# Holding the row gathers of a routed-expert stage behind the dot products of two groups back

## The chip, the core and the metric

One core of one Trainium2 chip runs one program. The metric is the time of one execution on the device in microseconds; the numbers given are medians of several executions.

## What is computed

The reference runs two transformer-like blocks over 256 tokens of width 1024. The part that the change touches is the feed-forward layer of the first block: each token has 8 heads, each head picks 16 of 16384 experts, and each expert is one row of 1024 numbers in a table `peer_u` and one in a table `peer_v`.

```python
def peer_ffn(h, w_q, sub_keys, u_tab, v_tab):
    ...
    def one_block(hb):
        ...
        idx = jnp.take_along_axis(cand_i, pos, axis=-1)
        g = jax.nn.softmax(top_s, axis=-1)
        u = u_tab[idx]
        act = jax.nn.gelu(jnp.einsum('thkd,td->thk', u, hb))
        wts = (g * act.astype(jnp.float32)).astype(hb.dtype)
        v = v_tab[idx]
        return jnp.einsum('thk,thkd->td', wts, v)
```

## The kernel before

The program has four stages: the first block up to its attention and recurrent branches (to about 390 us), the expert-row stage described below (about 390 to 1170 us), the dense part of the second block (to about 1450 us), and a loop over 32 dense experts (to the end). Each engine has its own instruction list, and semaphores tie them together.

The expert-row stage works on *rows*. A row here is one pick of one head for all 128 tokens of a tile: 128 partitions times 1024 numbers of `peer_u`, and as much of `peer_v`, together 1 MB. There are 2 tiles x 8 heads x 16 picks = 256 rows, and this text counts them 0 to 255 in the order in which they are gathered. Four rows are a *group* (`GROUP = 4`), so there are 64 groups, 0 to 63; group G holds the rows 4G to 4G+3. There are 16 buffers (`uv_rows[k]`), one for each pick k of a head; row r uses buffer r mod 16.

For each row:

- POOL (GpSimd) waits until the matmuls of row r-16 have used the buffer (`s_pv`, named `v_rows_used`), then issues two indirect DMAs, one for the u half (L709) and one for the v half (L711). Both count on `uv_full[k]`.
- DVE (`dot_rows`, L1806) waits for both halves and takes the dot product of the u half with the token rows. The last dot of a group counts on `s_dots`.
- ACT (`gelu_dots`, L1164) takes the GELU of the group's four dots, DVE (`weights`, L1813) multiplies by the softmax weights, and ACT (`diagonals`, L1173) writes four diagonal matrices.
- PE (L905) multiplies each diagonal by the v half of its row and adds into PSUM, and counts on `s_pv`.

POOL runs this as a loop, `Fori`, of 4 iterations for each tile; an iteration is two heads, that is 32 rows. A head begins with a copy of its 16 indices (L697). DVE's loop over the same 32 rows is written so that it also chooses the experts for two later heads, in pieces set between the dots: `best_keys` (L1561, L1564, L1568, L1581), `best_pairs` (L1600), `soften` (L1611, L1612), `part_of_route` (L1622 to L1627). Each piece is a few short instructions with a drain between them, and stands between the dots of a group and the multiplication by the weights of that same group. The dots of the next group stand after that multiplication.

At the change of tile ACT also copies the finished tile out of PSUM (L1342).

```python
dot_rows(tile, 0, 1, i)
best_keys(after, 1)
weights(tile, 0, 1, i)
dot_rows(tile, 0, 2, i)
best_pairs(0)
weights(tile, 0, 2, i)
```

What orders POOL against DVE before the change is only `s_pv`: POOL may be up to 16 rows ahead of PE, whether or not DVE has taken their dots.

Of the kernel before, what the change touches and what calls it, by code (L numbers as in the profile page):

```python
# [35 lines left out]
PH, PK, TOPK = 8, 128, 16  # L36
# [9 lines left out]
SLOT = 4096  # L46
RING = 5
GROUP = 4
N_BANKS = 8


# [78 lines left out]
def banks_first(plan):  # L130
# [5 lines left out]
    for job in plan:  # L136
# [12 lines left out]
        else:  # L149
            at[job] = turns["early"] % N_BANKS  # L150
            turns["early"] += 1
# [83 lines left out]
class Jobs:  # L235


    def __init__(self, plan, banks, full, free, earlier=None):

        self.full, self.free = full, free  # L240
        self.base = [earlier.base[b] + earlier.uses[b] if earlier else 0 for b in range(N_BANKS)]
        self.uses = [0] * N_BANKS
        self.place = {}
# [18 lines left out]

    def all_free(self, eng, banks=range(N_BANKS)):
        for b in banks:
            eng.wait_ge(self.free[b], self.base[b] + self.uses[b])
# [41 lines left out]
def build_program(nc, a, out):  # L307
# [6 lines left out]
    with ExitStack() as ctx:  # L314
        def sem(name):
            return ctx.enter_context(nc.semaphore(name))
# [97 lines left out]
        last_row = {0: 8, 1: 15, 2: 10, 3: 12, 4: 14}  # L414
        n_groups = TOPK // GROUP

# [151 lines left out]
        s_dots = sem("dots_ready")  # L568
# [98 lines left out]
        def _(pool):  # L667
# [21 lines left out]
            for tile in range(TT):  # L689
                per = 2 * (2 + TOPK)  # L690
                with pool.Fori(0, PH // 2) as i:
                    own.enter(i, per)
                    for par in range(2):
                        g = tile * PH + par
                        pool.wait_ge(s_pv, i * (2 * TOPK) + TOPK * g + 1)
                        own.mark(pool.wait_ge(s_route, i * 2 + g + 1))  # L696
                        own(pool.tensor_copy(idx_now[:, par, :].bitcast(U32), route_idx[:, par, :].bitcast(U32)))  # L697
                        pool.sem_inc(s_taken, 1)
                        for k in range(TOPK):
                            for s, place in first_row.items():  # L700
                                if k == place:
                                    unit_free(pool, last_in_slot(s, n_first))
                            if k == 2:
                                unit_free(pool, last_in_slot(1, n_first) - RING)
                            if k == 3:
                                A.filled(pool, "ss2")
                            own.mark(pool.wait_ge(s_pv, i * (2 * TOPK) + TOPK * g + k + 2))
                            at_k = bass.IndirectOffsetOnAxis(ap=idx_now[:, par, k:k + 1].bitcast(U32), axis=0)
                            pool.indirect_dma_start(out=uv_rows[k][:, 0:D], out_offset=None, in_=a["peer_u"],  # L709
                                                    in_offset=at_k).then_inc(uv_full[k], 16)  # L710
                            pool.indirect_dma_start(out=uv_rows[k][:, D:2 * D], out_offset=None, in_=a["peer_v"],  # L711
                                                    in_offset=at_k).then_inc(uv_full[k], 16)
                own.leave(PH // 2)
# [30 lines left out]
        def _(pe):  # L744
# [163 lines left out]
            for tile in range(TT):  # L908
# [3 lines left out]
                with pe.Fori(0, PH // 2) as i:  # L912
                    for par in range(2):
                        g = tile * PH + par
                        for k in range(TOPK):
                            if k % GROUP == 0:
                                pe.wait_ge(s_diag, i * (2 * n_groups) + g * n_groups + k // GROUP + 1)
                            add(ps[:, 2 * tile, :], diag[par][:, k, :], uv_rows[k][:, D:D + 512])
# [233 lines left out]
        def _(act):  # L1152
# [7 lines left out]

            def gelu_dots(tile, par, j, i):
                some = slice(j * GROUP, (j + 1) * GROUP)
                act.wait_ge(s_dots, i * (2 * n_groups) + (tile * PH + par) * n_groups + j + 1)
                fn(dots[:, par, some], dots[:, par, some], ACT.Gelu_apprx_tanh,  # L1164
                   scale=rcol[:, 4 * tile:4 * tile + 1]).then_inc(s_act, 1)

            def diagonals(tile, par, j, i):
                g = tile * PH + par
                act.wait_ge(s_wts, i * (2 * n_groups) + g * n_groups + j + 1)
                if j == 0:  # L1170
                    act.wait_ge(s_pv, i * (2 * TOPK) + TOPK * g + 1)
                for k in range(j * GROUP, (j + 1) * GROUP):
                    last = fn(diag[par][:, k, :], ident, ACT.Copy, scale=wts[:, par, k:k + 1])  # L1173
                last.then_inc(s_diag, 1)

            for job in plan_first("ACT"):
                kind, i = job[0], job[1] if len(job) > 1 else 0
# [22 lines left out]
                elif kind == "rg":  # L1200
                    A.filled(act, *job)
                    n, j = i // 2, i % 2
# [143 lines left out]
            for job in plan_second():  # L1346
                kind, i = job[0], job[1] if len(job) > 1 else 0
# [145 lines left out]
        def _(dve):  # L1493
            own = Own(dve, s_v)
            ts, tt, stt = dve.tensor_scalar, dve.tensor_tensor, dve.scalar_tensor_tensor

            dve.wait_ge(s_cols, 16)
            dve.wait_ge(s_const, 1)
            def small_chains():
# [144 lines left out]
            for job in plan_first("DVE"):  # L1644
                kind, i = job[0], job[1] if len(job) > 1 else 0
# [113 lines left out]
                elif kind in ("brr", "bra"):  # L1759
                    if i == 0:  # L1760
                        dve.wait_ge(s_gate, KD)
                    g = 2 * i + (KD if kind == "brr" else 0)
# [39 lines left out]
            def dot_rows(tile, par, j, i):  # L1802
                g = tile * PH + par
                for k in range(j * GROUP, (j + 1) * GROUP):
                    dve.wait_ge(uv_full[k], i * 64 + 32 * (g + 1))
# [104 lines left out]
            for job in plan_second():  # L1910
                kind, i = job[0], job[1] if len(job) > 1 else 0
# [81 lines left out]
                elif kind in ("bra", "brc"):  # L1993
                    if i == 0:
                        dve.wait_ge(s_gate, KD + KD)
                    g = 2 * i + (KD if kind == "bra" else 0)
# [92 lines left out]
            with dve.Fori(0, total) as q:  # L2089
# [6 lines left out]
                g, u = g_act, u_act  # L2096
# [132 lines left out]
```

## Time and profile before

| | |
|---|---|
| median of 3 runs | 2408.35 us (2406.23 to 2408.68) |
| the profiled execution | 2423.89 us |
| its span in the trace | 2422.1 us |
| mean granted TensorE clock | 0.939 of full speed |
| busy over the span | PE 86%, PEld 49%, DVE 40%, ACT 23%, POOL 21% |
| HBM read | 782.55 MB, 324 GB/s over the span |
| gathers (queue q0) | 268.47 MB in 512 indirect DMAs |

Read busy shares by stage: the shares of the whole span mix stages that have different limits. "issue" as the releaser of an idle time means that the profile shows nothing that the engine waited for. In a timeline each row is one instruction or several merged ones, with the idle time before it in brackets.

### The profile page before, as it was taken

The numbers are of one execution on the slowest core, as the hardware profiler recorded it, in microseconds if no ns is written. First come the engines' busy times: TensorE is split into PE (matmuls) and PEld (weight loads), VectorE is DVE, ScalarE is ACT, GpSimd is POOL, SyncE is SP. The second block draws the span as 40 slices with busy tenths as digits, with TensorE's granted clock in tenths as the row PEclk, the third lists the DMA queues.
The fourth block names the chain that finished last, engine by engine and source line by source line (L and its number), as shares of the span: only waits on it lengthen the run. The fifth ranks groups of instructions, "written<-read, shape, count | busy, mean of one in ns | idle before, by whom it ended". The sixth has DMA issues, their size and how long they took to land.

```text
span 2422.1 us, 27077 instructions
## 1 busy us (share of the span) xinstructions
PE 2085.5 (86%) x8940; PEld 1175.5 (49%) x8941; DVE 971.1 (40%) x2238; ACT 568.9 (23%) x1046; POOL 499.0 (21%) x560
## 2 busy tenths in 40 slices
PE   8998998977467577487799969999999999999997
PEld 7867887622223233132478854444444444444443
DVE  5955555655566565364175241211111111111113
ACT  4635301311112111021215222222222222222221
POOL 0000003466666666566100000000000000000000
PEclk9999999988789787798899979999999999999999
DMA  7352486799999999899632419699999999999995
GB/s 296 134 214 80 190 359 258 289 367 355 356 366 359 351 362 375 338 350 359 268 146 105 174 44 413 257 429 428 429 429 429 428 428 429 429 428 429 429 429 219
DMA packets 111685, 784.31 MB, mean 324 GB/s; under 512 B 13040, under 2 KB 13296, under 8 KB 80144
## 3 DMA queue, kind: packets, MB, share of 16 engines
q1 hardware_dynamic: 37904, 515.18, 51.4%
q0 software_dynamic: 73728, 268.47, 29.1%
q8 instruction: 28, 0.46, 0.1%
q14 instruction: 25, 0.20, 0.0%
HBM read 782.55 MB, written 1.05 MB: 324 GB/s over the span
## 4 chain that ended last, share of the span: by engine, by line
PE 75%; issue 11%; DVE 6%; ACT 2%; DMA 2%; another core or an unknown queue 2%; POOL 1%; DVEq 0%; ACTq 0%; POOLq 0%; SPq 0%
PE ps L746 57%; PE ps L905 15%; DVE ring L1806 2%; PE ps L1105 1%; DMA ring<-in_peer_v,arena 1%; PE ps L878 1%; POOL ring L709 1%; DVE arena L1806 1%; POOL ring L711 1%; DMA arena<-in_peer_v,arena 1%; DVE arena L1564 0%; ACT arena L1173 0%; DVE arena L1755 0%; PE ps L1136 0%
## 5 line engine op out<-in xcount | busy, mean ns | idle before, releaser
L746 PE MATMUL ps<-ring,arena 128*64 128x512 f32 (+2 forms) x3336 | 747.5, 588 | 40.7 <-issue 40.7
L905 PE MATMUL ps<-ring,arena 128*128 128x512 f32 x768 | 373.2, 640 | 155.0 <-issue 105.8
L746 PEld LDWEIGHTS ps<-ring,arena 128*64 128x64 f32 (+1 forms) x3336 | 262.1, 140 | 499.0 <-issue 498.4
L746 PE MATMUL ps<-arena,ring 128*128 128x256 f32 x2208 | 493.0, 383 | 7.5 <-ACT arena L1367 3.7
L746 PEld LDWEIGHTS ps<-arena,ring 128*128 128x128 f32 x2208 | 420.5, 191 | 73.5 <-issue 11.4
L905 PEld LDWEIGHTS ps<-ring,arena 128*128 128x128 f32 x768 | 154.9, 206 | 369.1 <-issue 314.7
L2101 DVE TENSOR_TENSOR arena<-ps,arena 128x512 f32<-128x512 f32 x66 | 45.7, 692 | 652.6 <-PE ps L1105 652.6
L1470 ACT COPY arena<-ps 128x512 f32<-128x512 f32 (+1 forms) x198 | 108.4, 548 | 727.7 <-PE ps L746 671.6
L1806 DVE CUSTOM_DVE_ANT_0 ring<-ring,ps 128x1024 f32<-128x1024 f32 x192 | 229.0, 1218 | 118.5 <-DMA ring<-in_peer_v,arena 106.0
L905 PE MATMUL ps<-arena 64*128 64x512 f32 (+2 forms) x568 | 204.5, 613 | 73.7 <-issue 38.1
L746 PE MATMUL ps<-arena 128*128 128x128 f32 (+6 forms) x1486 | 221.6, 305 | 28.5 <-DVEq L2077 13.6
L746 PEld LDWEIGHTS ps<-arena 128*128 128x128 f32 (+2 forms) x1486 | 196.6, 198 | 45.6 <-issue 22.1
L709 POOL DMA_INDIRECT ring<-in_peer_u,arena x192 | 182.5, 950 | 145.2 <-issue 63.1
L711 POOL DMA_INDIRECT ring<-in_peer_v,arena x192 | 180.2, 939 | 59.8 <-issue 54.3
L905 PEld LDWEIGHTS ps<-arena 128*128 128x128 f32 (+1 forms) x568 | 81.3, 197 | 171.2 <-issue 129.4
L1173 ACT ACTIVATE arena<-arena 128x128 f32<-128x128 f32 x256 | 81.8, 391 | 204.3 <-issue 131.2
L1164 ACT ACTIVATE arena<-arena 128x4 f32<-128x4 f32 x64 | 19.1, 298 | 368.2 <-issue 250.4
L1806 DVE CUSTOM_DVE_ANT_0 arena<-arena,ps 128x1024 f32<-128x1024 f32 x64 | 76.4, 1219 | 35.9 <-DMA arena<-in_peer_v,arena 31.1
L697 POOL COPY arena<-arena 128x16 uint32<-128x16 uint32 x16 | 3.3, 206 | 387.5 <-POOLq L696 387.5
L709 POOL DMA_INDIRECT arena<-in_peer_u,arena x64 | 60.1, 939 | 52.4 <-PE ps L905 21.6
L711 POOL DMA_INDIRECT arena<-in_peer_v,arena x64 | 60.2, 941 | 19.6 <-issue 18.7
L1541 DVE CUSTOM_DVE_ANT_0 ring<-ring,arena 128x1024 f32<-128x1024 f32 x48 | 56.0, 1222 | 3.0 <-DVE arena L1709 0.7
(330 smaller groups left out, 1172.7 us busy)
## 6 DMA issues: line engine op xcount, KB each, us to landing
ring<-in_w_exp SPq DMA_DIRECT2D x192, 2048.0 KB, 17.1
ring<-in_w_in SPq DMA_DIRECT2D x24, 2048.0 KB, 7.8
ring<-in_w_ada SPq DMA_DIRECT2D x12, 2048.0 KB, 8.6
ring<-in_w_out SPq DMA_DIRECT2D x4, 2048.0 KB, 8.2
ring<-in_w_peer_q SPq DMA_DIRECT2D x4, 2048.0 KB, 10.5
ring<-in_w_br_rnn SPq DMA_DIRECT2D x4, 1280.0 KB, 7.6
ring<-in_w_br_attn SPq DMA_DIRECT2D x2, 2048.0 KB, 13.7
ring<-in_peer_u,arena POOLq DMA_INDIRECT x192
```

The lines of the kernel that those rows point to most:

```text
L709: pool.indirect_dma_start(out=uv_rows[k][:, 0:D], out_offset=None, in_=a["peer_u"], in_offset=at_k).then_inc(uv_full[k], 16)
L711: pool.indirect_dma_start(out=uv_rows[k][:, D:2 * D], out_offset=None, in_=a["peer_v"], in_offset=at_k).then_inc(uv_full[k], 16)
L746: return pe.matmul(o, l, r, start=start, stop=stop)
L878: last = pe.matmul(ps[:, b, j * P:(j + 1) * P], w[:, c, j * P:(j + 1) * P], hT[:, c, i * P:(i + 1) * P], start=(c == 0 and j == 0), stop=( ...
L905: return pe.matmul(o, l, r, start=start, stop=False, skip_group_check=True)
L1105: last = pe.transpose(ps[:, EXPERT_BANK[job], j * P:(j + 1) * P], z_sb[:, n, j * P:(j + 1) * P], ident)
L1164: fn(dots[:, par, some], dots[:, par, some], ACT.Gelu_apprx_tanh, scale=rcol[:, 4 * tile:4 * tile + 1]).then_inc(s_act, 1)
L1173: last = fn(diag[par][:, k, :], ident, ACT.Copy, scale=wts[:, par, k:k + 1])
L1470: own(act.copy(dst, src))
L1541: own.mark(dve.tensor_tensor_reduce(w[:, j, :], w[:, j, :], c_row, 1.0, 0.0, ALU.mult, ALU.add, mod[:, m:m + 1]))
L1806: last = dve.tensor_tensor_reduce(uv_rows[k][:, 0:D], uv_rows[k][:, 0:D], h2_rows[tile], 1.0, 0.0, ALU.mult, ALU.add, dots[:, par, k:k + 1])
L2101: own(tt(dst.rearrange("p j (h s) -> p j h s", h=2), ps[:, bank, :].rearrange("p (j h s) -> p j h s", j=4, h=2), bias.unsqueeze(3).to_broa ...
```

## The change

POOL gets one more wait at the head of every group of four rows: the gathers of group G wait until the dots of group G-2 are done. `s_dots` is the semaphore on which DVE counts one for each group. So that the first two groups wait for nothing, and no wait is for zero, DVE adds 2 (`AHEAD`) to it at its start, and ACT's waits on the same semaphore are raised by 2.

```diff
 GROUP = 4
+AHEAD = 2
 N_BANKS = 8
...
                             if k == 3:
                                 A.filled(pool, "ss2")
+                            if k % GROUP == 0:
+                                pool.wait_ge(s_dots, i * (2 * n_groups) + g * n_groups + k // GROUP + 1)
                             own.mark(pool.wait_ge(s_pv, i * (2 * TOPK) + TOPK * g + k + 2))
                             at_k = bass.IndirectOffsetOnAxis(ap=idx_now[:, par, k:k + 1].bitcast(U32), axis=0)
                             pool.indirect_dma_start(out=uv_rows[k][:, 0:D], out_offset=None, in_=a["peer_u"],
...
             def gelu_dots(tile, par, j, i):
                 some = slice(j * GROUP, (j + 1) * GROUP)
-                act.wait_ge(s_dots, i * (2 * n_groups) + (tile * PH + par) * n_groups + j + 1)
+                act.wait_ge(s_dots, AHEAD + i * (2 * n_groups) + (tile * PH + par) * n_groups + j + 1)
...
             ts, tt, stt = dve.tensor_scalar, dve.tensor_tensor, dve.scalar_tensor_tensor
 
+            dve.sem_inc(s_dots, AHEAD)
             dve.wait_ge(s_cols, 16)
```

On POOL, the place between the fourth and the fifth row of a head (the end of a group and the head of the next), before the change. `v_rows_used` is `s_pv`; `bank_full_2` is a wait that matters only for the first head.

```order
L707 REGISTER_ALU [waits bank_full_2]
L709 DMA arena<-in_peer_u,arena 128x1024 [waits v_rows_used]
L711 DMA arena<-in_peer_v,arena 128x1024
L707 REGISTER_ALU
L709 DMA arena<-in_peer_u,arena 128x1024 [waits v_rows_used]
L711 DMA arena<-in_peer_v,arena 128x1024
```

The same place after the change (all line numbers are 3 higher there). `dots_ready` is `s_dots`.

```order
L710 REGISTER_ALU [waits bank_full_2]
L712 DMA arena<-in_peer_u,arena 128x1024 [waits v_rows_used]
L714 DMA arena<-in_peer_v,arena 128x1024
L709 REGISTER_ALU
L710 REGISTER_ALU [waits dots_ready]
L712 DMA arena<-in_peer_u,arena 128x1024 [waits v_rows_used]
L714 DMA arena<-in_peer_v,arena 128x1024
```

One register instruction and one wait have come in at the head of the group; no gather has moved past another. On DVE, PE and SP the rows are the same in the same order; ACT has four more register instructions.

The start of a head on POOL, before the change.

```order
L696 ISA [waits v_rows_used]
L697 COPY arena<-arena 128x16 [waits peer_routes_ready]
L279 ISA
L707 REGISTER_ALU [waits pool_own]
L709 DMA ring<-in_peer_u,arena 128x1024 [waits v_rows_used]
L711 DMA ring<-in_peer_v,arena 128x1024
```

And after it.

```order
L697 ISA [waits v_rows_used]
L698 COPY arena<-arena 128x16 [waits peer_routes_ready]
L280 ISA
L709 ISA [waits pool_own]
L710 REGISTER_ALU [waits dots_ready]
L712 DMA ring<-in_peer_u,arena 128x1024 [waits v_rows_used]
L714 DMA ring<-in_peer_v,arena 128x1024
```

The copy of the indices stays ahead of the new wait.

## Rows read from the trace of the kernel before

**Rows 1.** The page, queue of the gathers: packets, MB, share of 16 engines.

```profile
q0 software_dynamic: 73728, 268.47, 29.1%
```

**Rows 2.** Windows, first to last gather: PE, PEld, DVE, ACT, POOL, clock, DMA share, GB/s.

```profile
392.00:1154.00 762.00, 535.28 (x1301) 249.14 (x1300) 434.76 (x1087) 128.64 (x353) 485.98 (x527) 0.85 0.92 350
```

**Rows 3.** Timeline of POOL, start of row 240's head: start, length, instruction, idle before.

```profile
1104.65 0.21 POOL L697 COPY arena<-arena 128x16 uint32<-128x16 uint32 x1
1105.84 0.97 POOL L709 DMA_INDIRECT ring<-in_peer_u,arena  x1 [0.97 <-issue]
```

**Rows 4.** Timeline of DVE, end of group 58, two before row 240's.

```profile
1102.09 0.08 DVE L1806 DVE_READ_ACCUMULATOR2_ANT arena<- 128x1 f32 x1
```

**Rows 5.** Timeline of DVE and POOL around rows 52 and 55 (groups 11 and 13).

```profile
554.36 0.93 POOL L709 DMA_INDIRECT arena<-in_peer_u,arena  x1 [0.30 <-issue]
...
561.62 0.08 DVE L1806 DVE_READ_ACCUMULATOR2_ANT arena<- 128x1 f32 x1
...
566.74 0.09 DVE L1564 MATCH_VALUE_LOAD arena<-arena 128x8 f32 x1 [4.37 <-issue]
...
567.44 0.94 POOL L709 DMA_INDIRECT ring<-in_peer_u,arena  x1 [5.93 <-PE ps L905]
```

**Rows 6.** Windows of 2 us, the one in which that idle time ends.

```profile
565.00:567.00 2.00, 2.00 (x6) 0.95 (x5) 0.26 (x2) 0.30 (x1) 0.00 (x0) 1.00 0.48 191
```

**Rows 7.** Timeline of DVE and POOL around rows 80 and 84 (groups 18 and 20).

```profile
634.84 0.97 POOL L709 DMA_INDIRECT ring<-in_peer_u,arena  x1 [0.97 <-issue]
...
644.85 0.20 DVE L1581 CAST arena<-arena 128x64 f32<-128x64 uint32 x1 [10.76 <-issue]
...
651.66 0.08 DVE L1806 DVE_READ_ACCUMULATOR2_ANT arena<- 128x1 f32 x1
...
653.14 0.93 POOL L709 DMA_INDIRECT arena<-in_peer_u,arena  x1 [8.64 <-PE ps L905]
```

**Rows 8.** Timeline of DVE and POOL around rows 108 and 109 (groups 25 and 27).

```profile
717.43 0.94 POOL L709 DMA_INDIRECT ring<-in_peer_u,arena  x1 [0.31 <-issue]
...
724.13 0.08 DVE L1806 DVE_READ_ACCUMULATOR2_ANT arena<- 128x1 f32 x1
...
725.02 0.94 POOL L709 DMA_INDIRECT ring<-in_peer_u,arena  x1 [5.42 <-PE ps L905]
```

**Rows 9.** Timeline of DVE, ACT and POOL around rows 140 and 144 (groups 33 and 35).

```profile
809.13 0.94 POOL L709 DMA_INDIRECT ring<-in_peer_u,arena  x1 [0.30 <-issue]
...
821.55 1.07 ACT L1342 COPY arena<-ps 128x512 f32<-128x512 f32 x2 [35.22 <-remote]
...
827.50 0.08 DVE L1806 DVE_READ_ACCUMULATOR2_ANT arena<- 128x1 f32 x1
...
828.73 0.96 POOL L709 DMA_INDIRECT ring<-in_peer_u,arena  x1 [4.02 <-POOLq L707]
```

**Rows 10.** Timeline of DVE and POOL around rows 180 and 183 (groups 43 and 45).

```profile
927.84 0.94 POOL L709 DMA_INDIRECT arena<-in_peer_u,arena  x1 [0.30 <-issue]
...
934.14 0.08 DVE L1806 DVE_READ_ACCUMULATOR2_ANT arena<- 128x1 f32 x1
...
940.67 0.93 POOL L709 DMA_INDIRECT ring<-in_peer_u,arena  x1 [5.63 <-PE ps L905]
```

**Rows 11.** Timeline of DVE and POOL around rows 208 and 212 (groups 50 and 52).

```profile
1007.73 0.97 POOL L709 DMA_INDIRECT ring<-in_peer_u,arena  x1 [0.97 <-POOL arena L697]
...
1022.23 0.20 DVE L1581 CAST arena<-arena 128x64 f32<-128x64 uint32 x1 [10.04 <-issue]
...
1027.65 0.08 DVE L1806 DVE_READ_ACCUMULATOR2_ANT arena<- 128x1 f32 x1
...
1029.12 0.94 POOL L709 DMA_INDIRECT arena<-in_peer_u,arena  x1 [11.73 <-PE ps L905]
```

**Rows 12.** Windows of 2 us around the end of that idle time of DVE.

```profile
1020.00:1022.00 2.00, 0.00 (x0) 0.00 (x0) 0.00 (x0) 0.00 (x0) 0.00 (x0) 0.50 0.91 361
1022.00:1024.00 2.00, 0.00 (x0) 0.00 (x0) 1.20 (x3) 0.80 (x3) 0.00 (x0) 0.50 0.01 4
```

## The prediction

> **What bounds the kernel now.** I read first the page and then the stage as a whole. The change touches only the stage in which rows are gathered: 512 indirect DMAs with 268.47 MB [rows 1]. From the first gather to the last it takes 762 us, about a third of the span, with the DMA engines 92% busy at 350 GB/s and POOL at 485.98 us, 64% [rows 2]. PE and DVE have room (535.28 and 434.76 of 762 us), so what sets the end of the stage is when the 256 rows are issued and moved.
>
> Then the timeline of POOL. One gather takes 0.94 us and 0.30 us of idle lies before it [rows 10], so a row of two gathers takes 2.48 us, and the first row of a head 0.88 us more: 0.21 us for the copy of the indices and 0.97 us of idle in place of 0.30 [rows 3]. 256 x 2.48 plus 15 x 0.88 is 648 us. The stage takes 762, so POOL stands for 114 us in all. That is the account that the change draws on: every microsecond that POOL is held and that no later stand takes up lengthens the kernel, because the DMA engines at 92% cannot catch it up.
>
> What does POOL stand for? Row 84 and row 212 wait for PE to free a buffer, 8.64 and 11.73 us [rows 7, 11]. The other stands are of another kind. Row 55 starts after 5.93 us, put down to PE, but the row that it overwrites had been used long before; it starts at 567.44, and the DMA engines fall from full to 0.48 in the window of 565 to 567 us [rows 5, 6]. DVE, between two short instructions of its choosing work with nothing to wait for, resumes at 566.74 in that same window [rows 5]. Again at row 212: DVE stands 10.04 us and resumes at 1022.23, where the DMA share falls from 0.91 to 0.01 [rows 11, 12]. So DVE and POOL at times stand for something that is behind the gathers in the DMA engines. That bears on the change twice: these stands make the dots late, and a POOL that is held lets the queue run empty.
>
> **The change, part by part.** The instruction that DVE adds at the start, the 4 register instructions of ACT and POOL's 64 waits with their register instructions cost nothing where they are met: POOL's next instruction is decoded under the 0.94 us of a running gather [rows 10]. Uncovered they would cost at most the extra idle of a head's start, 0.67 us (0.97 less 0.30), and that is what I add, rounded up to 0.9 us, from the last dot to the gather where POOL is really held. Behind the waiting POOL stand only gathers, and behind them DVE's dots, ACT's diagonals and PE.
>
> Which of the 64 waits hold POOL? I set the end of each group's last dot beside the start of the gather two groups later. Where DVE keeps up there is slack: group 58 ends at 1102.17 and row 240 starts at 1105.84, 3.7 us later [rows 3, 4]; 44 groups have a slack like that, from 0.7 us up, and the first two wait for nothing. In 18 the gather starts before the dots end, and they lie in six clusters, each behind a long stand of DVE (or ACT) inside the choosing work. In each the hold that the later rows of the cluster can't make good is what counts:
>
> 1. Row 52. Group 11's dots end at 561.62 + 0.08 = 561.70; the gather could start at 562.6, not 554.36: **+8.2 us** [rows 5]. The stand of row 55, 5.93 - 0.30 = 5.6 us, comes after it and may be taken up: +2.6.
> 2. Row 80. Dots to 651.74, gather at 652.6 instead of 634.84. But row 84 waits for PE to 653.14 anyway; four rows and more after 652.6 it starts at 662.6: **+9.4** [rows 7]. If the queue runs empty, DVE's stand of 10.76 us ends earlier. In rows 11 and 12 the queue is empty 5.8 us after the last gather: row 211's second one starts three rows and 1.24 us after 1007.73, at 1016.4, and the share is down at 1022.2. With POOL held at row 80, its last gather is row 79's second, 2.12 us (0.94 + 0.21 + 0.97) before 634.84, the queue is empty at 638.5, DVE resumes there and not at 644.85, and row 84 comes 6.3 us earlier: +3.1.
> 3. Row 108. Dots to 724.21, gather at 725.1 instead of 717.43: **+7.7**; if the stand of row 109 (5.42 - 0.30) is taken up, +2.6 [rows 8].
> 4. Row 140, at the change of tile. Dots to 827.58, gather at 828.5 instead of 809.13: +19.3. Row 144 started at 828.73, with 8.8 us of stands between the two (19.6 us less 9.9 for four rows and 0.9 for the head). If these are taken up, +10.6. DVE waited here for ACT, idle 35.22 us to 821.55; if ACT too resumes when the queue is empty (5.8 us after 807.9, so 813.7), +2.7 [rows 9].
> 5. Row 180. Dots to 934.22, gather at 935.1 instead of 927.84: **+7.3**; +2.0 if the stand of row 183 (5.63 - 0.30) is taken up [rows 10].
> 6. Row 208. Dots to 1027.73, gather at 1028.6 instead of 1007.73; row 212 at 1038.6 instead of 1029.12: +9.4. With an emptied queue (5.8 us after 1005.6, so 1011.4) DVE's stand of 10.04 us falls away, row 208 comes at 1018.6 and row 212 at 1028.6: 0 [rows 11].
>
> Upper sum, nothing shortened or taken up: 8.2 + 9.4 + 7.7 + 19.3 + 7.3 + 9.4 = 61 us. Lower sum, everything: 2.6 + 3.1 + 2.6 + 2.7 + 2.0 + 0 = 13 us. I take the long stands of places 2 and 6 as shortened, because rows 6 and 12 show two stands that end with the queue, and POOL's own as mostly staying, because they fall behind gathers freshly issued, not behind the wait: 8.2 + 3.1 + 7.7 + 8 (between the ends of place 4) + 7.3 + 0 = 34 us.
>
> Here a rule speaks about the size. By the Trainium skill, page "DMA: Bandwidth & Descriptors", section "Queues, rings and completion order", each DMA engine takes turns between the queues that have work, a packet at a time, so a small transfer of another queue should not wait for the whole queue of the gathers. By that rule a held POOL shortens nothing and the sum would be the upper one, 61 us; rows 6 and 12 speak against it, with two cases only.
>
> The profiled execution took 2423.89 us, 1.8 more than its span of 2422.1, and the median of the runs shown is 2408.35, 0.64% less; the stands may be somewhat shorter without a profile. Profiled I expect 2423.9 + 34 = 2458; as a median 2408.35 + 34 x about 0.95 = **2441 us**.
>
> **The rivals.** (a) *Nothing is shortened*: DVE and ACT stand as long as before, whatever the queue holds. Then the upper sum: 2408.35 + 61 = 2469. For it: most of the stands, as the 10.76 us one, ended while gathers were still under way [rows 7]. Against it: rows 6 and 12. Chance 0.12.
>
> (b) *Taken up*: the holds fall where POOL would have stood anyway. The 114 us of stands are enough to take 13 to 61 us. For it: rows 84 and 212 started when PE released them, and whatever else they might have stood for was hidden. Against it: places 1, 3 and 5 hold POOL before its stand, not in it. It gives 2408 to 2413. Chance 0.14.
>
> (c) *Faster*: with a queue that runs empty sooner DVE's stands in the choosing work fall so much that the dots, and behind them PE, are no longer late. Then the two waits for a buffer go, 8.64 + 11.73 less twice 0.30, 19.8 us: 2408.35 - 19.8 = 2388.6. The point from which it decides: group 18's dots must end by 634.8 and not at 651.74, so 17 of the 20 us for which DVE stands at place 2 must go, and as much at places 4 and 6. For it: under the change POOL is held and the queue empties at exactly these places. Against it: the two groups that may be issued ahead are eight rows, 8 x 2.48 = 20 us of gathers, so the queue is as full as before when the first long stand of a place begins. Chance 0.14.
>
> (d) *The forecast*, +13 to +55 us: 0.60.
>
> **How the numbers follow.** No change and a change of under 0.2%, 5 us, can't be told apart. The likeliest is (d) with 2441, its own range 2421 to 2463. (d) and (a) are slower: 0.72. (b) lies mostly within 0.2%: 0.13 for the same, the rest slower or faster by a little. (c) and a rest of (b) give 0.15 for faster. The range of 8 in 10 leaves out (c) and, above, the part of (a) beyond 2467: 2402 to 2467.
>
> **What the profile of the changed kernel would show.** Right: POOL's gathers of rows 52, 80, 108, 140, 180 and 208 start about 0.9 us after the last dot of the group two back, with DVE as releaser; the stage from first to last gather takes 790 to 800 us, and the DMA share in it falls to about 0.89; DVE's idle times of 10 us at places 2 and 6 occur once each and not twice; after the stage every stage keeps its length. Wrong in size: the second long stand stays (then 61 us), or POOL's stands of 3 to 6 us between gathers vanish behind the new waits (then 13 us or nothing). Wrong in sign: rows 80, 140 and 208 start as early as before because DVE's stands there are gone, and rows 84 and 212 start without waiting for PE.

## The result, and the profile after

The changed kernel takes 2415.43 us (median of 20 executions, 2404.43 to 2424.51), the kernel before beside it on the same chip 2403.11 us (20 executions, 2399.03 to 2409.62). The ratio is 1.0043, with a 95% interval of 1.0031 to 1.0055: slower by 10 us by the ratio (7 to 13), by 12.3 us between the medians. The forecast of 2441 us had the sign and the way in which POOL is held, and was 26 us too high. Of these, 5.2 us are the base (2408.35 us were shown, 20 executions gave 2403.11) and 20 us are the sum: 32.6 us were added, 12.3 measured. That is also less than the 13 us of the forecast's own lower sum, and more than the 5 us at most of rival (b). One execution further below, 2462.74 us of the late kernel without the change, was in a slower state and is left out of its median.

The page of the changed kernel's profiled execution (2418.26 us), span, DVE and POOL, and the queue of the gathers:

```profile
span 2416.5 us, 27154 instructions
...
PE 2103.3 (87%) x8940; PEld 1183.1 (49%) x8941; DVE 973.8 (40%) x2238; ACT 569.2 (24%) x1046; POOL 499.1 (21%) x560
...
q0 software_dynamic: 73728, 268.47, 29.1%
```

Windows of it: first to last gather, then what follows (columns as in [rows 2]).

```profile
392.00:1152.00 760.00, 549.99 (x1295) 254.31 (x1294) 437.48 (x1084) 128.65 (x353) 485.35 (x527) 0.85 0.92 351
...
1152.00:1450.00 298.00, 268.81 (x1198) 213.55 (x1198) 130.46 (x306) 83.15 (x145) 11.50 (x17) 0.94 0.40 147
1450.00:2416.00 966.00, 910.60 (x4784) 408.44 (x4780) 171.20 (x374) 210.94 (x298) 0.00 (x0) 0.99 0.95 405
```

The same two later stretches in the kernel before:

```profile
1154.00:1452.00 298.00, 263.22 (x1179) 210.50 (x1179) 130.28 (x304) 82.51 (x144) 10.93 (x16) 0.93 0.39 145
1452.00:2422.00 970.00, 913.55 (x4797) 409.44 (x4792) 171.33 (x374) 211.35 (x299) 0.00 (x0) 0.99 0.95 403
```

The stage takes 760 us, as [rows 2] had it (762), and not the 790 to 800 that were expected; the DMA share is 0.92 and not 0.89. That reads as "no change", but the execution in [rows 2] took 2423.89 us, 21 us above the median of its own kernel, and this one 2418.26, 3 us above its own. One profile of each can't show a difference of 12 us here. What it can show is which idle times there are.

Row 172 of the changed kernel (group 43, which waits for the dots of group 41), timeline of DVE, ACT and POOL:

```profile
905.61 0.94 POOL L714 DMA_INDIRECT ring<-in_peer_v,arena  x1 [0.30 <-issue]
908.06 0.16 DVE L1817 TENSOR_TENSOR arena<-arena 128x4 f32<-128x4 f32 x1 [9.46 <-issue]
...
912.71 0.08 DVE L1810 DVE_READ_ACCUMULATOR2_ANT arena<- 128x1 f32 x1
...
912.83 0.30 ACT L1167 ACTIVATE arena<-arena 128x4 f32<-128x4 f32 x1 [3.21 <-DVE arena L1810]
...
913.67 0.94 POOL L712 DMA_INDIRECT ring<-in_peer_u,arena  x1 [7.13 <-PE ps L908]
```

The last dot ends at 912.79, and the gather starts 0.88 us later. That distance, which was forecast as 0.9 us, is what identifies a hold. The name behind the arrow doesn't: it says PE, since PE's semaphore was the last to count by the profile, though the row of PE that is needed had been done long before. The hold is 7.13 - 0.30 = 6.8 us. Behind it is a stand of DVE, 9.46 us to 908.06, in which DVE waits for nothing that is shown; the four dots come after it. Row 204 reads the same:

```profile
998.78 0.93 POOL L714 DMA_INDIRECT ring<-in_peer_v,arena  x1 [0.30 <-issue]
1002.59 0.17 DVE L1817 TENSOR_TENSOR arena<-arena 128x4 f32<-128x4 f32 x1 [9.45 <-issue]
...
1007.24 0.08 DVE L1810 DVE_READ_ACCUMULATOR2_ANT arena<- 128x1 f32 x1
...
1008.20 0.93 POOL L712 DMA_INDIRECT ring<-in_peer_u,arena  x1 [8.49 <-PE ps L908]
```

Besides these, rows 52 and 108 are held, 9.4 and 6.8 us: 31.3 us in four places. Rows 80, 140, 180 and 208, which the forecast named, are not held in this execution.

### The profile page after: what moved, and what is told of

The parts are those of the page before. It is cut to its first block, busy times and chain, and to the rows that moved or that the text cites. A ratio compares the mean times of both kernels' runs of the same rounds, so it can differ in the third digit from the quotient of the medians.

```text
span 2416.5 us, 27154 instructions
## 1 busy us (share of the span) xinstructions
PE 2103.3 (87%) x8940; PEld 1183.1 (49%) x8941; DVE 973.8 (40%) x2238; ACT 569.2 (24%) x1046; POOL 499.1 (21%) x560
## 3 DMA queue, kind: packets, MB, share of 16 engines
HBM read 782.55 MB, written 1.05 MB: 324 GB/s over the span
## 4 chain that ended last, share of the span: by engine, by line
PE 77%; issue 12%; DVE 4%; POOL 3%; ACT 2%; DMA 2%; DVEq 0%; another core or an unknown queue 0%; POOLq 0%; ACTq 0%; SPq 0%
PE ps L749 57%; PE ps L908 17%; DMA ring<-in_peer_v,arena 2%; PE ps L1108 1%; POOL ring L712 1%; POOL ring L714 1%; PE ps L881 1%; POOL arena L714 1%; POOL arena L712 0%; DVE ring L1810 0%; DVE arena L1759 0%; PE ps L1139 0%; ACT arena L1270 0%; DVEq L1559 0%; ACT arena L1176 0%
## 5 line engine op out<-in xcount | busy, mean ns | idle before, releaser
L908 PE MATMUL ps<-ring,arena 128*128 128x512 f32 x768 | 383.6, 655 | 151.4 <-issue 122.6
## 6 DMA issues: line engine op xcount, KB each, us to landing
ring<-in_w_peer_q SPq DMA_DIRECT2D x4, 2048.0 KB, 10.6
```

The source lines that it names most:

```text
L908: return pe.matmul(o, l, r, start=start, stop=False, skip_group_check=True)
```

## The account of POOL

For every profiled execution I took the start of each of the 512 gathers and subtracted the bare issue that the prediction found (1.24 us a gather, 0.88 us more at a head). What is left is POOL's idle time beyond issue. I sorted it: up to row 16 (23 to 26 us in all profiles of this kind, about the loads of the stage before); holds (the gather starts 0.75 to 1.05 us after the last dot of the group it waits for); waits for a buffer (the gather starts as closely behind PE's matmuls of 16 rows back); and the rest, POOL's own stands. Beside it stand DVE's idle times over 1.3 us behind group 0 that don't end in a dot product. "Ahead" is the number of groups that POOL may be ahead of the dots. Lines without a number are from the chip of the result; the second, third and fourth chip are those of 2404, 2411 and 2416 us below.

```
kernel (chip)         ahead  holds  buffer  own    all    DVE    time of the
                                    waits   stands  POOL   stands profiled one
before                  -     0      22.8    63.5   109.8  131    2423.9
before again (3rd)      -     0       0.6    75.3   100.7  117    2410.8
no wait in POOL (3rd)   -     0      14.0    68.2   109.0  129    2420.2
AHEAD 4 (3rd)           4     0      17.7    67.2   110.0  110    2417.0
AHEAD 3 (4th)           3     0       7.2    71.1   104.1  132    2415.8
value added on PE (3rd) 2    17.1     0      65.8   111.0   85    2420.3
the change              2    31.3     0      51.8   108.3   81    2418.3
the change (2nd)        2    31.3     0      49.0   107.3   79    2414.4
the change (4th)        2    24.5     0      62.5   112.5   94    2420.8
AHEAD 1 (4th)           1   (413)     0             445.0    0    2758.4
before (quiet chip)     -                            13.7     0    2324.7
```

In each line the time less "all POOL" is 2307 to 2314 us. Issue and idle time together are the length of the stage, so this says that what lengthens the stage passes whole into the time, and that nothing before or behind it takes it up. With two groups ahead there are 17 to 31 us of holds, and against that no buffer waits (0 to 22.8 without the bound or with three and four ahead) and mostly less of POOL's own stands: 49 to 66 us against 64 to 75. In three of these four profiles some gathers of a group's head start 1.6 to 2.4 us behind the dots, most in the two with the smaller holds; they are counted as own stands and may be holds in part.

The totals differ by less than the medians: 109.8 us on average with two ahead, 106.7 in the five lines without the bound or with three and four. But the five profiled executions took 7.6 us more than the medians of their kernels on average (20.8, 0.2, 8.4, 8.1 and 0.4 us), and the four lay at theirs (0.1 us above on average). With that, 3.1 + 7.5 = 10.6 us are left for the bound, near the 10 to 12 measured.

## Experiments

The experiments ran on five chips. On three the kernel before takes 2403.87, 2410.61 and 2415.91 us; on two, called quiet below, 2323.83 and 2324.58 us.

### On the quiet chip: before, half of the change, four groups ahead, and the start value on PE

The kernel before once more, and three variants. The half keeps DVE's increment and ACT's raised waits and leaves out POOL's:

```diff
-                            if k % GROUP == 0:
-                                pool.wait_ge(s_dots, i * (2 * n_groups) + g * n_groups + k // GROUP + 1)
```

The second has another constant, the third adds the value on PE:

```diff
-AHEAD = 2
+AHEAD = 4
```

```diff
+            pe.sem_inc(s_dots, AHEAD)
...
-            dve.sem_inc(s_dots, AHEAD)
```

> The kernel before, unchanged, for a second profile. The first one was of an execution of 2423.9 us, 20 us above the median of its 20 runs (2403.1). If DVE's long stands in the choosing work are fixed by the place in its instruction list, this profile shows them at the same places (groups 10, 17, 24, 32, 42, 48/49) and the stage from first to last gather takes about 760 us. If they depend on chance, such as how full the gather queue is at the time, their number and places differ and the stage can be 740 to 750 us. Time 2400 to 2412 us either way.

> The change without POOL's waits: DVE's one added instruction and ACT's raised waits alone. Theory 1 (the loss comes from holding POOL): same as before, ratio 1.000 (2403 us), holds of rows 52, 108, 172, 204 gone. Theory 2 (the loss, or the changed pattern of DVE's stands, comes from DVE's instructions standing one place later): ratio 1.003 to 1.006, and DVE's stands at the places of the changed kernel (one of 9.5 us behind L1572 in groups 25, 41 and 49) and not the double ones of the kernel before.

> All instructions of the change, but the gathers of a group wait for the dots of four groups back, which the wait for the buffer implies already. Theory 1: POOL is never held by the new wait, ratio 1.000 to 1.001. Theory 3 (the 64 waits themselves, or POOL's longer instruction list, cost the time): ratio 1.003 to 1.006.

> The change with the starting value of dots_ready added by PE instead of DVE, so that DVE's instruction list is exactly that of the kernel before, and POOL has its waits. Theory 1: ratio as the change, 1.004 (2415 us). Theory 2: DVE's stands return to the places of the kernel before, where two of 10 us follow each other (groups 17 and 49), and rows 80 and 208 are held by 6 to 18 us: ratio 1.008 to 1.014.

The expected 2400 to 2412 us for before did not come: its profiled execution took 2324.68 us. Measured against before (2323.83 us, 29 executions): the half 1.0002 (0.9988 to 1.0016), four ahead 1.0011 (0.9997 to 1.0025), and the whole change with the value added on PE 0.9992 (0.9978 to 1.0006). All three are the same as before, and the reason is in the windows of the kernel before on this chip, first to last gather:

```profile
389.00:1054.00 665.00, 538.76 (x1298) 248.31 (x1296) 441.41 (x1084) 126.95 (x348) 486.73 (x527) 0.91 1.01 400
```

The stage takes 665 us and not 762, at 400 GB/s, with the DMA engines full. The instructions are the same; POOL's idle time beyond issue is 13.7 us, and DVE has no stand in its choosing work. Without stands the dots are never late and the waits never bind. So the waits by themselves, their register instructions and ACT's cost nothing that can be measured, as the prediction had it. But the chip could not tell which part costs on the others, and the same kernels had to run there.

### On a chip of 2404 us: the change, and DVE made late on purpose

In three kernels DVE also takes three maxima over 128x4096 numbers, 13.3 us (4.42 each), in six loop iterations. Their result isn't used (4.42 us is the time of one in the trace of the late kernel with the change).

```diff
                     best_keys(after, 1)
+                    for _ in range(3):
+                        done(dve.tensor_reduce(hot[:, 0, 0:1], all_scores.rearrange("p r k -> p (r k)"), AX, ALU.max))
```

> The change as it is, on the chip of this job. In the second profile of the kernel before, neither DVE nor POOL stands in the stage (664 us from first to last gather). Theory 1 (the change costs only where DVE is late by more than eight rows are ahead): without stands the ratio is 1.000 (0.999 to 1.001) and the stage as long as before; with stands as in the first profile 1.003 to 1.006. Theory 3 (the waits cost by themselves): 1.004 on any chip.

> The kernel before, with DVE made late on purpose: three extra maximum reductions over 128x4096 numbers (about 4.3 us each, some 13 us) in every one of the 6 loop iterations, between the dots of the second group of the iteration and the multiplication by the weights. Results are not changed by it. Theory 1: the 16 buffers cover 13 us; ratio 1.000 to 1.002 where there are no other stands, DVE catches up in the next groups.

> The same 13 us of lateness in each of 6 iterations, with the change. Theory 1: POOL has 8 rows less the 3 that are under way, some 12 us, before the wait holds it; from one group's dots to the next one's are 2.4 + 13 + 4.7 + 0.9 = 21 us, so each iteration holds POOL by 6 to 9 us: 36 to 52 us in all, ratio 1.015 to 1.023 (2360 to 2375 us where before takes 2324). Theory 2 or 3: no more than f_change, 1.000 to 1.004.

> The same lateness, with the gathers held behind the dots of three groups back instead of two. Theory 1: four more rows are 10 us more of cover, so POOL is held by nothing or by under 1 us in each iteration: ratio 1.000 to 1.003. A loss of 0.7 times f_late_change or more would speak for a cost of the waits that is not a matter of how far ahead they let POOL go.

Measured: the change 2414.95 us, 1.0036 (1.0020 to 1.0052). Late without the change 2426.94 us, 1.0083 (1.0056 to 1.0110); late with it 2464.75 us, 1.0251 (1.0223 to 1.0280); late with three groups ahead 2446.31 us, 1.0189 (1.0160 to 1.0218). The windows of the late one with the change, over the same stretch as above:

```profile
392.00:1152.00 760.00, 502.70 (x1219) 236.36 (x1217) 489.18 (x1050) 120.77 (x328) 450.61 (x490) 0.83 0.86 326
```

DVE is 52 us busier than in the changed kernel, the DMA share is 0.86, and 490 POOL instructions lie in the stretch in place of 527. POOL is held 77 us in this profile against 31. So the same change costs 38 us instead of 11 between the medians (40 instead of 9 by the ratios) when DVE is late by 13 us more in each iteration: the price of the change rises with how late the dots are.

Two expectations failed. The 16 buffers do not cover the 13 us: the late kernel without the change is 23 us slower, and its profiled execution has 46 us of buffer waits, 24 of them before row 116, behind two stands of DVE of 10.27 and 9.35 us that come on top. And three groups ahead were to cost at most 1.003. Their median is 19 us above that of the late kernel without waits, with intervals of the two ratios that don't overlap, though POOL is held only 3 us in the profiled execution. That execution took 2434.4 us, 12 us under its kernel's median, and has as much idle time of POOL (125 us) as that of the late kernel without waits (127 us, 2438.9 us), so it doesn't show where the 19 us lie; that stays open. The mark set beforehand for a cost of the waits themselves, 0.7 times the loss of the late change, is passed if both are counted from before (0.0189 of 0.0251); counted from the late kernel without waits it is half. That the waits themselves cost nothing rests on the runs without late dots, here above and in the next two sections.

### On a chip of 2411 us: the parts again, where DVE stands

> The kernel before once more. Two kinds of chip have shown up: one on which it takes 2403 us and one on which it takes 2324. On a chip of the first kind: time 2398 to 2413 us, POOL's idle time beyond the bare issue of the gathers 90 to 105 us in all (110 in the first profile, of an execution of 2424 us), and no stand of 20 us at the change of tile. On one of the second kind: 2318 to 2329 us and 10 to 15 us.

> DVE's added instruction and ACT's raised waits alone, no wait on POOL. On a chip of the first kind, theory 1: 1.000 (0.999 to 1.001). Theory 2 (DVE's list moved by one instruction changes its stands): 1.003 or more, or 0.997 or less. Second kind: 1.000.

> All instructions of the change, waits for the dots of four groups back. On a chip of the first kind, theory 1 (only being held costs): 1.000 to 1.001, no gather starts 0.9 us behind a last dot. Theory 3 (the waits and the longer list cost by themselves): 1.003 to 1.005, like the change. On the second kind 1.000 to 1.001 again.

> The change with DVE's list left as before (PE adds the starting value). On a chip of the first kind, theory 1: as the change there, 1.0036 to 1.0043. Theory 2: 1.008 to 1.014 with DVE's stands at the places of the kernel before. Second kind: 0.999 to 1.001.

Measured against before (2410.61 us): without POOL's waits 0.9995 (0.9979 to 1.0012); with all waits and four groups ahead 1.0002 (0.9982 to 1.0022); with all waits, two ahead and the value added on PE 1.0037 (1.0019 to 1.0055). The cost is there only when POOL may be held, whichever engine adds the start value. That the moved list of DVE, ACT's registers or the waits as instructions cost something is ruled out to about 5 us, the upper ends of these intervals.

### On a chip of 2416 us: one, two and three groups ahead

> The change with AHEAD = 1: the gathers of group G wait for the dots of group G-1, so that four rows at most are issued ahead. On the chips of about 2405 us the change costs 8 to 13 us: POOL is held about 31 us and the other stands shrink by about 20. Theory A (a stand of DVE ends when the queue of gathers is empty, so a queue that runs empty more often shortens them): POOL is held at most group heads of which DVE takes its choosing work between two groups, at least 100 us in all, but DVE's idle times of over 1.3 us inside the choosing work fall clearly below the 80 us that they have under the change, to 50 or less, and no idle time of DVE there reaches 6 us. Theory B (the shrinking under the change was chance, the stands have nothing to do with the queue): they are 80 to 130 us as in every other kernel, and the time is higher by the whole hold. In numbers: A 2440 to 2480 us, B 2490 to 2560. On a chip without stands both give the bare effect of a short queue, and only the hold is read.

> The change with AHEAD = 3: twelve rows at most are issued ahead of the dots. With AHEAD = 4 no time was lost (1.0002), with 2 about 10 us. If the cost comes only from POOL being held, it depends on by how much DVE is late: under AHEAD = 2 the gathers of a held group began 5 to 9 us after they could have; one group more is 10 us of gathers, so no hold is left and the time is that of before, 0.998 to 1.002. The rival is that part of the cost comes from having the wait at all (then 1.002 to 1.003).

> The change again on the same chip as the two beside it: 1.0036 to 1.0043 of before on a chip of about 2405 us, with POOL held 31 us in four places; 1.000 on a chip of about 2324 us, where no engine stands.

Measured against before (2415.91 us): one ahead 2763.81 us, 1.1455 (1.1418 to 1.1491); three ahead 2415.40 us, 1.0005 (0.9983 to 1.0028); the change 2422.73 us, 1.0045 (1.0029 to 1.0062), with 24.5 us of holds in three places and not 31 in four.

The times expected for one ahead, 2440 to 2560 us by either theory, were far too low. What it said of DVE's stands was right for theory A: none is left. A group with one ahead, timeline of DVE and POOL:

```profile
838.31 0.94 POOL L712 DMA_INDIRECT ring<-in_peer_u,arena  x1 [7.26 <-DVE arena L1810]
...
847.04 0.94 POOL L714 DMA_INDIRECT ring<-in_peer_v,arena  x1 [0.30 <-issue]
...
853.23 1.22 DVE L1810 CUSTOM_DVE_ANT_0 ring<-ring,ps 128x1024 f32<-128x1024 f32 x1 [1.27 <-DMA ring<-in_peer_v,arena]
854.38 0.08 DVE L1810 DVE_READ_ACCUMULATOR2_ANT arena<- 128x1 f32 x1
...
855.34 0.94 POOL L712 DMA_INDIRECT ring<-in_peer_u,arena  x1 [7.37 <-DVE arena L1810]
```

From the first gather of a group to the next group's is 17.03 us: 8.73 to the start of the group's last gather, 6.19 until its row has landed and DVE begins the dot, 1.23 for the dot, 0.88 to the gather. Issue alone takes 9.92 us, so POOL is held 7.1 us in every group even when DVE is never late. The account has 59 holds behind row 16, of 6.2 to 7.9 us, 413 us in all, 7.0 each; the shorter ones are at the heads, where the copy of the indices falls into the hold. The step in the expectation that failed was the round trip of a group: it had been taken as hardly longer than the issue. From it comes an estimate that the prediction lacked. With A groups ahead the slack of a hold is A x 9.92 - 17.03 us: -7.1, 2.8, 12.7 and 22.6 us for one to four. It takes the dots as late by the whole stand, which holds for a DVE that was just in time. With two ahead a stand of 9.46 us then is 6.7 us too much; row 172 was held 6.8, and so was row 108 behind a stand of the same length. Row 204 was held 8.2, since DVE had stood 3.55 us shortly before as well, and row 52 9.4, behind four stands of 2.0 to 4.5 us. With three ahead the stand of 9.46 us is covered, and the time is that of before.

Between the last dot at 854.38 us and the next group's, DVE does its choosing work without a stand, there and in every other group of this execution.

### Slower pace without a wait for the dots

In the kernel before, POOL clears one element behind the two gathers of every row and waits for that (in one variant behind every second row, in another two elements).

```diff
                                                     in_offset=at_k).then_inc(uv_full[k], 16)
+                            own(pool.memset(iota_i[:, 0:1], 0.0))
```

> The kernel before, with a one-element memset of POOL (and a wait for its end) behind the two gathers of every second row: POOL issues a little more slowly and nothing waits for the dots. A row of two gathers takes 2.48 us bare and 2.59 us on the chip of 2324 us, where the DMA engines are full, so a memset of some 0.3 us for every second row brings POOL just to the pace at which the transfers are done. Theory A (the stands of DVE and POOL come from gathers issued faster than they are moved): the stands begin to shrink, the stage gets 10 to 60 us shorter on a chip of about 2405 us. Theory B (they come at these chips whatever the pace): the time is that of before to 1% above.

> The same behind every row, some 0.3 to 0.4 us a row: 2.8 to 2.9 us a row, so the DMA engines have room. Bare the stage would take 256 x 2.85 + 14 = 744 us against 752 to 761 in the profiles of before on such chips. Theory A: the stands of DVE in its choosing work fall from 110 to 132 us to 20 us or less, POOL's own from 63 to 73 us likewise, and the time is that of before or up to 20 us less. Theory B: the stands stay and the time rises by 60 to 90 us.

> Two memsets and one wait behind every row: some 3.0 us a row. Both theories give a longer stage; A with hardly any stand (256 x 3.0 + 14 = 782 us, +20 to 30 us against before), B with all of them (+130 us).

These came to a quiet chip (before 2324.58 us), where no engine stands, and so the question was not answered. Measured: 2411.24, 2499.39 and 2508.36 us, 1.038, 1.076 and 1.080. A clear with its wait costs 87 us for 128 of them and 175 us for 256, 0.68 us each, twice what the expectation took. The timeline of POOL with a clear behind every row shows why:

```profile
605.48 0.94 POOL L711 DMA_INDIRECT ring<-in_peer_v,arena  x1 [0.31 <-issue]
606.41 0.12 POOL L713 MEMSET arena<- 128x1 f32 x1
607.41 0.93 POOL L709 DMA_INDIRECT ring<-in_peer_u,arena  x1 [0.88 <-POOLq L707]
```

0.12 us are the instruction, and the next gather starts after 0.88 us of idle and not 0.30, since it waits for POOL's own last instruction. It is the same 0.9 us as behind a hold, and bears out that term of the prediction.

## Why the prediction was right, and where it was wrong

**Right.** What lengthens the stage of the gathers lengthens the kernel: the account's constant of 2307 to 2314 us. The waits cost nothing where they are met (1.0011 and 1.0002 with four ahead, beside 1.0002 and 0.9995 without POOL's waits). A held gather follows the last dot by 0.88 us (forecast 0.9). Holds stand behind long stands of DVE. What follows the stage keeps its length: 966 us for what took 970. Rival (c), faster, did not come, and the upper sum of rival (a) neither. Rival (b), taken up, came for the greater part: 17 to 31 us of holds cost 10 to 12.

**The step that failed** is the sum over the places, 34 us, above all its term for POOL's other stands, which were taken as mostly staying. The holds alone came near it, 26 us on average and 31.3 in two of four profiles; what was not subtracted is 24 us of other idle time that went. In detail:

First, the places were taken as fixed. What [rows 5] and [rows 7 to 11] show is where one execution stood. The changed kernel was held at rows 52, 108, 172 and 204 in one execution and at 44, 76, 108 and 140 in another. What recurs is the place in the loop: 11 of the 13 holds in the four profiles with two ahead are at the row 12 of an iteration (44, 76, 108, 140, 172, 204), which waits for the group behind the first call of `best_keys`, and in that call or close behind it DVE stands in every iteration. Place 4, for which 8 us were taken and 19.3 stood in the upper sum, came from ACT's 35.22 us at the change of tile [rows 9]. In these two executions ACT stood 13 and 11 us there; in the other two with two groups ahead it stood 25 and 28 us, and row 140 was held 8.8 and 11.0 us. Row 144 also waited for PE (3.0 us, its gather starts 0.81 us behind the matmuls), which the prediction had read for rows 84 and 212 alone.

Second, "POOL's own as mostly staying". They shrank, from 64 to 75 us to 49 to 66, and the waits for a buffer [rows 7, 11] are gone: in the four profiles with two groups ahead none was left. By the means of the account (buffer and own 81.5 us without a bound or with three and four ahead, 57.3 with two) that is 24 us, against holds of 26 us. The difference of 2 us, and the 3 us of the totals, are too small, since the profiled executions of those five kernels lay 7.6 us above the medians, as said at the account; with that they come to about 11. A profiled execution can lie 20 us off its median, so this is a balance of means and no more exact than that.

Third, the reason given for the stands of places 2 and 6, that a stand ends when the queue is empty. Its consequence came true. The long stands between the short instructions of L1561 to L1581, which come second at places 2 and 6 [rows 7, 11] (there in the second call, `best_keys(after, 1)`), number five or six over 5 us in each of the five profiles without holds; with two groups ahead there are none in three profiles and two in the fourth. But the condition is too narrow. Windows of the changed kernel around the end of the stand at 1002.59 us:

```profile
1000.00:1002.00 2.00, 0.00 (x0) 0.00 (x0) 0.00 (x0) 0.00 (x0) 0.00 (x0) 0.50 1.02 406
1002.00:1004.00 2.00, 0.00 (x0) 0.00 (x0) 1.41 (x4) 1.13 (x4) 0.00 (x0) 0.50 1.00 399
1004.00:1006.00 2.00, 1.80 (x2) 0.84 (x3) 2.00 (x3) 0.15 (x1) 0.00 (x0) 0.50 0.10 39
```

DVE resumes with the DMA engines full, and they run empty some 2 us later. In all eleven stands over 5 us in the first two profiles of the change the engines are full when DVE resumes. In the five profiles without holds it is otherwise for 13 of 45, which end in 2 us in which the share is under 0.95, as in [rows 12]. One of them, in before on the third chip, windows and timeline of DVE:

```profile
755.00:757.00 2.00, 0.00 (x0) 0.00 (x0) 0.00 (x1) 0.15 (x1) 0.00 (x0) 1.00 0.62 246
757.00:759.00 2.00, 0.00 (x0) 0.00 (x0) 1.54 (x8) 0.00 (x0) 0.94 (x2) 1.00 0.00 0
...
757.00 0.09 DVE L1564 MATCH_VALUE_LOAD arena<-arena 128x8 f32 x1 [7.84 <-issue]
```

So a stand can end before the queue is empty, but none was seen to last beyond it: in the nine profiles of the account on the slower chips with two groups ahead, with more or without a bound, no stand over 5 us goes on for more than 0.5 us once at most one packet of a gather is under way. In the five without holds DVE stands 593 us in all and the queue is empty in this sense for 145 us, 4% of the stage; under 2 us of the two coincide, where 24 would by chance. In part this is so by construction, since the queue also runs empty while POOL waits behind a DVE that is at its dots.

What the holds do seems to come after the first stand: the DMA engines then have a gap, and the second stand doesn't happen. Over the profiles of the account on chips of this kind the sum of DVE's stands orders itself by the groups ahead without an overlap: 110 to 132 us with three or more or no bound, 79 to 94 with two, none with one. The late kernels don't keep this order (80 us without a bound, 94 with three ahead, 87 with two). That fewer gathers under way mean fewer stands is shown for the kernels without added work, and clearest by the one with one group ahead. That the gap in the DMA engines is the means was only argued; with one ahead DVE also has idle times of 5 us before its work, in which something may have been made ready. The kernels of the slower pace were to tell that apart and did not.

By the Trainium skill, page "Runtime: NRT & Kernel Launch", section "Instruction fetch mechanics", an engine fetches its instructions over a DMA queue of its own in large blocks, mostly hidden, and a taken branch outside what it holds costs a stall. It would fit an engine that stands with nothing to wait for in a loop. The trace shows no such fetch. The queues of the changed kernel from 546 to 780 us, a stretch with stands of 6.4 and 9.5 us:

```profile
DMA packets 22652, 82.49 MB, mean 353 GB/s; under 512 B 2515, under 2 KB 2515, under 8 KB 22652
## 3 DMA queue, kind: packets, MB, share of 16 engines
q0 software_dynamic: 22652, 82.49, 92.0%
```

Not one packet of an instruction queue is recorded in it, so as far as the records go these stands are not the fetch of instructions. But only two instruction queues, with 54 packets, are recorded in the whole execution, and not of which engines they are, so this speaks against the fetch and doesn't rule it out. What the stands are stays open, and so does why some chips have none.

The rule that the prediction weighed, that a DMA engine takes turns between the queues, stood for rival (a) and its 61 us. It was right in that a stand's end doesn't need an empty queue. Its 61 us failed all the same, since the second stands and POOL's other idle time fell away.

## What to carry to other kernels

A bound on how far one engine may run ahead has a slack that can be worked out before any run: groups ahead times the issue of a group, less the round trip of one group (issue, landing, work, release). Here that is 2.8 us for two groups and 12.7 for three. A hold is about the length of a stand less this slack. The kernel loses less than its holds (10 to 12 us for 26 here), because other idle time of the same engine goes. Three groups, with more slack than a single stand of 9.5 us, cost nothing that was measured in this kernel; with DVE late on purpose they cost 19 us that no profile explains. And when stands have no cause in the profile, take their number and size from several executions, never their places from one, and ask whether the change that adds waits also removes waits of the same engine: count all of its idle time, not only the new part.

## What the runs showed of the hardware

The same kernel takes 2323.83 and 2324.58 us on two chips and 2403.11 to 2415.91 us on the others (that of the result and three more), and all of the difference lies in the stage of the gathers: 664 us from first to last against 752 to 761. On the slower ones both engines stand with nothing to wait for that is recorded, DVE for up to 11 us at a time and POOL mostly for 2 to 6, in sum about 120 and 70 us without the bound; on a quiet chip neither does, with the same gathers at 400 GB/s. There the parts of the change that were run, the whole of it but for the engine that adds the start value among them, cost nothing, so a measurement there alone would have called it free.
